# Hybrid pooling and mLSTM block on one core: pool weights folded into the input projection, gates stacked, row broadcasts in one matmul

## What is computed

```python
h = rms_norm(x, norm_g) * (1 + scale) + shift            # scale, shift, gate from silu(c) @ w_ada + b_ada
proj = h @ w_in                                          # 1024 x (7 * 512 + 8): u, z_pool, q, k, v, o, z_mlstm, gates
pool_out = causal_pool_mixer(u, w_pool, ls_pool) * silu(z_pool)
q, k = split(silu(causal_depthwise_conv(proj_qk)))
hm = mlstm_chunkwise(q, k, v, ig, lf)                    # 4 heads of 128, chunks of 128 positions
hm = hm * rsqrt(mean(hm * hm) + EPS) * mh_norm_g
mix = concat([pool_out, hm * sigmoid(o) * silu(z_mlstm)])
out = rms_norm(x + gate * (mix @ w_out), final_g)
```

## Time and profile before

| quantity | value |
|---|---|
| median of 3 runs | 2010.35 us (2009.97 to 2011.29) |
| profiled execution, its own time | 2011.44 us |
| span of its trace, first to last instruction | 2009.7 us |
| mean granted TensorE clock | 0.99 |
| PE busy | 1906.6 us (95%) |
| DVE busy | 1061.0 us (53%) |
| ACT busy | 469.8 us (23%) |
| POOL busy | 248.1 us (12%) |
| HBM read, written | 271.63 MB, 46.14 MB |

### The profile page before, as it was taken

One profiled execution on the slowest core, in us unless ns is written; L12 is line 12 of the kernel. 1 busy time (PEld: TensorE's weight loads), 2 busy tenths in 40 slices (PEclk: granted clock), 3 DMA queues, 4 the chain that ended last, 5 costly groups with the idle time before them and its releaser, 6 DMA issues.

```text
span 2009.7 us, 26240 instructions
## 1 busy us (share of the span) xinstructions
PE 1906.6 (95%) x9121; PEld 1554.7 (77%) x9121; DVE 1061.0 (53%) x2346; ACT 469.8 (23%) x979; POOL 248.1 (12%) x222
## 2 busy tenths in 40 slices
PE   2797799999999999999999999999999999999998
PEld 1585588788878888788877888778887888778886
DVE  7774476453754357362664527543474626545272
ACT  1232332112222122221222222211222122222221
POOL 0433322000030001200021000300012000210000
PEclk9998899999999999999999999999999999999999
DMA  8676562455225551456414553255513564245421
GB/s 286 205 245 198 197 232 72 161 197 200 95 92 193 192 186 53 150 193 209 148 66 154 193 197 110 91 185 195 188 64 130 196 209 147 84 142 194 168 84 63
DMA packets 120889, 319.58 MB, mean 159 GB/s; under 512 B 11356, under 2 KB 48948, under 8 KB 120756
## 3 DMA queue, kind: packets, MB, share of 16 engines
q1 hardware_dynamic: 120756, 317.81, 46.5%
HBM read 271.63 MB, written 46.14 MB: 158 GB/s over the span
## 4 chain that ended last, share of the span: by engine, by line
issue 52%; PE 21%; DVE 15%; DMA 5%; POOL 2%; ACT 1%; SPq 1%; DVEq 0%; POOLq 0%; ACTq 0%
PE ps_acc L407 5%; PE ps_acc L408 5%; PE ps_acc L409 5%; DMA sb_x_in<-x 2%; DVE sb_dmat L967 2%; DVE sb_k_w L967 1%; DMA sb_x_res<-w_out 1%; DVE sb_x_res L1370 1%; DMA sb_x_res<-x 1%; DVE sb_x_res L1383 1%; POOL sb_h_rs L873 1%; DMA out<-sb_x_res 1%; DVE sb_x_in L949 1%; DVE sb_acc_cv L1177 1%; DVE sb_mixm_lo L1284 1%
## 5 line engine op out<-in xcount | busy, mean ns | idle before, releaser
L407 PE MATMUL ps_acc<-sb_hT_hi,sb_w_split 128*128 128x512 f32 x1536 | 609.8, 397 | 28.1 <-DVE sb_oz L1194 16.1
L409 PE MATMUL ps_acc<-sb_hT_hi,sb_w_split 128*128 128x512 f32 x1536 | 603.4, 393 | 0.0
L408 PE MATMUL ps_acc<-sb_hT_lo,sb_w_split 128*128 128x512 f32 x1536 | 603.0, 393 | 0.0
L407 PEld LDWEIGHTS ps_acc<-sb_hT_hi,sb_w_split 128*128 128x128 f32 x1536 | 292.0, 190 | 90.4 <-DVE sb_oz L1194 17.8
L409 PEld LDWEIGHTS ps_acc<-sb_hT_hi,sb_w_split 128*128 128x128 f32 x1536 | 291.4, 190 | 62.6
L408 PEld LDWEIGHTS ps_acc<-sb_hT_lo,sb_w_split 128*128 128x128 f32 x1536 | 292.2, 190 | 58.7
L873 POOL TENSOR_TENSOR sb_h_rs<-sb_h_var,sb_mhalf 128x4 f32<-128x4 f32 x32 | 32.4, 1013 | 1149.7 <-DVE sb_h_var L1249 1149.7
L1177 DVE SCALAR_TENSOR_TENSOR sb_acc_cv<-sb_shifted,sb_par,sb_acc_cv 128x512 f32<-128x512 f32 x192 | 146.5, 763 | 6.8
L407 PE MATMUL ps_acc<-sb_wo_hi,sb_mixm_hi 128*128 128x512 f32 x256 | 107.0, 418 | 6.8 <-DVE sb_x_res L1370 3.5
L407 PE MATMUL ps_acc<-sb_wo_hi,sb_mixp_hi 128*128 128x512 f32 x256 | 101.1, 395 | 0.0
L408 PE MATMUL ps_acc<-sb_wo_lo,sb_mixp_hi 128*128 128x512 f32 x256 | 101.1, 395 | 0.0
(11 more groups left out here) (205 smaller groups left out, 2782.4 us busy)
## 6 DMA issues: line engine op xcount, KB each, us to landing
sb_w_split<-w_kept SPq DMA_DIRECT2D x392, 512.0 KB, 3.3
w_kept<-sb_w_split SPq DMA_DIRECT2D x56, 512.0 KB, 4.5
sb_x_res<-x SPq DMA_DIRECT2D x34, 512.0 KB, 5.7
out<-sb_x_res SPq DMA_DIRECT2D x32, 512.0 KB, 2.7
sb_x_in<-x SPq DMA_DIRECT2D x30, 512.0 KB, 5.7
sb_w_raw<-w_in SPq DMA_DIRECT2D x56, 256.0 KB, 3.4
sb_qT<-w_ada SPq DMA_DIRECT2D x4, 1024.0 KB, 6.4
sb_kT<-w_ada SPq DMA_DIRECT2D x4, 1024.0 KB, 5.4
```

What stands on the lines that cost most here:

```text
L407: pe.matmul(dst, st_hi, mv_hi, start=start, stop=False)
L408: pe.matmul(dst, st_hi, mv_lo, start=False, stop=False)
L409: return pe.matmul(dst, st_lo, mv_hi, start=False, stop=stop)
```

## The change

Five things change together.

1. The u columns of w_in are multiplied by w_pool once, in block 0 (the mean runs over positions, the map over channels, so the map can come first). Eight pieces f, two to a group: SP loads 256 KB of w_in (`load_fold`), PE turns four 128 x 128 blocks (`fold_transposed`, after tile 7+f) and multiplies them by w_pool (`fold_product`, after tile 8+f), ACT and DVE make the high and the low part, SP writes both to `w_kept` (`keep_fold`). In all blocks the u units then come from there, in block 0 too. `pool_map` goes away on PE, and `y_mixed(j)` reads the window sums straight from SBUF, in the same chunk, right after silu of zp(j). The tables TASK, SCO and the number of DVE steps follow.
2. In DVE's order `m_mixed(j-1)` comes after `y_mixed(j)` at the end of chunk j, and `y_low(j-1)` before `windows(j)`; on PE `hm_transposed(j-1)` comes after tile zp(j).
3. The gates' weights lie high beside low as 16 columns, and 16 matmuls a block replace 24; DVE adds the two halves.
4. A broadcast is one matmul of 512 columns: DVE lays out m and inter for the four heads side by side, each row kept only under its own head (`m_wide`, `inter_wide`, with `head_mask`), and a column of `chunk_sel` sums the four rows of chunk j.
5. The heads' output has a buffer of its own (it was `q_in`); `w_pool` lies in `q_in` and the raw gate weights in `v` until they are used; the ring has 5 slots, not 6; the loads of w_out stand six units earlier in SP's queue, and one load fewer stands between the first store of a block and the last load of the next block's x.

```diff
-RING = 6
+RING = 5
-hm = q_in
+hm = sb("hm", [P, NH, P])
-wpool = sb("wpool", [P, NH, P])
+wpool = q_in
...
+            def load_fold(f):
+                if f >= 2:
+                    sp.wait_ge(fold_T, f - 1)
+                off = OFF_U + P * (f // 2)
+                sp.dma_start(fold_raw[f % 2].rearrange("p (k n) -> p k n", n=P),
+                             w_in_v[:, 4 * (f % 2):4 * (f % 2) + 4, off:off + P]).then_inc(fold_loaded[f % 2], 16)
+            def keep_fold(f):
+                m = U_UNITS[f]
+                sp.wait_ge(fold_lo, f + 1)
+                for n, t in enumerate((mixm_hi, mixm_lo)):
+                    sp.dma_start(w_kept[m][:, n, :], t[:, f % 2, :, :].rearrange("p h t -> p (h t)").bitcast(F32)).then_inc(
+                        fold_kept[f % 2], 16)
...
-                wout_units = {V_UNITS + 2 * (WOUT_TILE + k) + 10: k for k in range(2, KT)} if first else {}
+                wout_units = {V_UNITS + 2 * (WOUT_TILE + k) + 4: k for k in range(2, KT)} if first else {}
...
-                        keep_w(m - RING + 1)
-                        load_raw(m)
+                        if m - RING + 1 in RAW_NO:
+                            keep_w(m - RING + 1)
+                        if m in RAW_NO:
+                            load_raw(m)
+                        else:
+                            f = U_UNITS.index(m)
+                            if m - RING in RAW_NO:
+                                kept_wait(m - RING)
+                            sp.wait_ge(fold_kept[f % 2], 32 * (f // 2 + 1))
+                            load_w(b, m)
+                        if m - 26 in range(2 * KT) and m % 2 == 0:
+                            load_fold((m - 26) // 2)
+                        if m - 33 in range(2 * KT) and m % 2 == 1:
+                            keep_fold((m - 33) // 2)
...
-                    for m in (UNITS + 2, UNITS + 3, UNITS + 4, UNITS + 5):
+                    for m in range(UNITS + 1, UNITS + RING):
                         load_w(b, m)
                     load_x(b + 1, 2)
                 store(b, 0)
                 if not last:
                     load_w(b, UNITS)
-                    load_w(b, UNITS + 1)
                     load_x(b + 1, 3)
...
-                    last = split3(sco[0:8, :], wg_hi[:, k, :], wg_lo[:, k, :], hT_hi[:, k, :], hT_lo[:, k, :],
-                                  k == 0, k == KT - 1)
+                    pe.matmul(sco[0:16, :], wg_split[:, k, :], hT_hi[:, k, :], start=k == 0, stop=False)
+                    last = pe.matmul(sco[0:16, :], wg_split[:, k, :], hT_lo[:, k, :], start=False, stop=k == KT - 1)
...
+                def fold_transposed(f):
...
+                    for i in range(4):
+                        last = pe.transpose(num[0][:, chunk(i)], fold_raw[f % 2][:, chunk(i)], ident)
+                def fold_product(f):
+                    pe.wait_ge(fold_T_copied, f + 1)
+                    if f:
+                        pe.wait_ge(fold_lo, f)
+                    for i in range(4):
+                        last = pe.matmul(num[1][:, chunk(i)], fold_turned[:, i, :], wpool[:, f // 2, :], start=True, stop=True)
...
-                    for h in range(NH):
-                        last = pe.matmul(bro[:, chunk(h)], col(row_sel, NH * j + h), m_hl[:, :], start=True, stop=True)
-                    last.then_inc(bro_full, 1)
+                    pe.matmul(bro[:, :], col(chunk_sel, j), m_wide[:, :, :].rearrange("p h t -> p (h t)"),
+                              start=True, stop=True).then_inc(bro_full, 1)
...
-                    if j > 0:
-                        pool_map(j - 1)
-                        hm_transposed(j - 1)
                     inter_rows(j)
                     tile("zp", j)
+                    if j > 0:
+                        hm_transposed(j - 1)
                     numerator_and_update(j)
-                pool_map(3)
...
+                for src, wide in ((m_row[0:16, :], m_wide), (inter_row, inter_wide)):
+                    step(V.tensor_tensor(wide[0:16, :, :], src.unsqueeze(1).broadcast_to([16, NH, P]),
+                                         head_mask[:, :].unsqueeze(2).broadcast_to([16, NH, P]), ALU.mult))
...
-                    V.scalar_tensor_tensor(silu_zp[:, :], src[:, :], ls2[:, g:g + 1], silu_zp[:, :], ALU.mult,
+                    V.scalar_tensor_tensor(silu_zp[:, :], acc_cv[:, HALO:], ls2[:, g:g + 1], silu_zp[:, :], ALU.mult,
...
-                        y_mixed(j - 1)
-                        m_mixed(j - 1)
...
-                    windows(j)
                     if j > 0:
                         y_low(j - 1)
+                    windows(j)
...
+                    y_mixed(j)
+                    if j > 0:
+                        m_mixed(j - 1)
                     if j >= 2 and not last_block:
                         prep_scale(b + 1, j - 2)
```

More of the change, by code:

```diff
@@ L91, in unit0 @@
     return V_UNITS + 2 * TILES.index((name, i))
+U_UNITS = [unit0("u", g) + half for g in range(4) for half in range(2)]
+RAW_UNITS = [m for m in range(UNITS) if m not in U_UNITS]
+RAW_NO = {m: n for n, m in enumerate(RAW_UNITS)}
+FOLD_TILE = 7
 def build(nc, x, c, norm_g, w_ada, b_ada, w_in, b_gates, conv_w, conv_b, w_pool, ls_pool, mh_norm_g,
@@ L463, in w_wait @@
                 def w_wait(m):
-                    if first:
-                        pe.wait_ge(w_lo_done, m + 1)
+                    if first and m in RAW_NO:
+                        pe.wait_ge(w_lo_done, RAW_NO[m] + 1)
                     else:
@@ L536, in one_block @@
                         gate_broadcast()
+                    if first and 0 <= t - FOLD_TILE - 1 < 2 * NH:
+                        fold_product(t - FOLD_TILE - 1)
+                    if first and 0 <= t - FOLD_TILE < 2 * NH:
+                        fold_transposed(t - FOLD_TILE)
                 def heads_to_scores(j):
@@ L563, in inter_rows @@
                     bro_wait(5 + 2 * j)
-                    for h in range(NH):
-                        last = pe.matmul(bro[:, chunk(h)], col(row_sel, NH * j + h), inter_hl[:, :],
-                                         start=True, stop=True)
-                    last.then_inc(bro_full, 1)
+                    pe.matmul(bro[:, :], col(chunk_sel, j), inter_wide[:, :, :].rearrange("p h t -> p (h t)"),
+                              start=True, stop=True).then_inc(bro_full, 1)
                 def numerator_and_update(j):
+                    if first and j == 0:
+                        pe.wait_ge(fold_lo, 2 * NH)
                     pe.wait_ge(sco_free, b * S_USES + (SCO["qk", j] + 1))
@@ L772, in one_block @@
                             wout_high(t - WOUT_TILE - 1)
+                    if first and 0 <= t - FOLD_TILE - 1 < 2 * NH:
+                        fold_high(t - FOLD_TILE - 1)
+                    if first and 0 <= t - FOLD_TILE < 2 * NH:
+                        fold_turn(t - FOLD_TILE)
                 def squares(j):
@@ L1390, in one_block @@
                 update_c(3)
-                y_mixed(3)
                 head_var(3)
```

125 lines of the change are left out of this document (85 added, 40 removed).

## The result

The changed kernel takes 1954.5 us (median of 4 runs, 1953.2 to 1955.8), against 2010.8 us for the kernel before in the same sessions: ratio 0.9718, 95% interval 0.9702 to 0.9733. The forecast was 1950.5, with a range from 1928 to 1978. The profiled execution took 1954.6 us with a span of 1952.7 us, so 57.0 us less than the span before.

The account below looks back on a forecast made before the run. PE was taken to bound seven blocks, weight traffic the first. Six loop blocks 36 us, the last 6.5 and block 0 17 sum to 59.5 off the profiled 2011.4, so a median of 1950.5 us, range 1928 to 1978.

Parts of the forecast that it names:

- Pool map, gates: On PE in each block: no pool map saves 3.44 us, 16 gate matmuls instead of 24 save 1.84 us.
- Broadcasts: On PE, eight times a block: one wide matmul of 0.24 us replaces four taking 0.48, saving 1.9 us a block.
- What DVE gives back: In chunks 2 and 3 PE waits for DVE, losing 0.5 and 1.4 us of each block's gain.
- The block's turn: Per block, out_m(1) no longer waits for y_mixed(3), 0.5 us; one weight load fewer on SP's queue, about 0.2.
- Block 0: First block gains 17 us: 8 up to the first scores, 9 from there to out_m(1); ends 5 and 29.
- the sum for the w_out laps: Block 0's load loop: laps fall from 11.9 to 8.6 us, raw load 3.8 of it; five laps save 16.6.
- The clock in block 0: PE in block 0 was costed at 0.23 us a matmul, 24 to a tile, 5.5 us a tile.
- DVE beside POOL: In block 0 POOL's splits might stretch y_mixed by up to 1.1 us in four chunks; nothing taken, far end 4.4.
- (B): Rival: DVE keeps up everywhere, block 0's loop runs at 6.7 us; 1928 us at the far end, 1932 middle; chance 0.19.
- (C): Rival: DVE paces the chunks, block 0 stays as it was because folds' traffic fills the DMA engines; 1978 us; chance 0.13.
- (D): Rival: slower, PE waits for weight loads with five ring slots; loads needing 11.6 us would eat 60 us; chance 0.04.
- (E): Rival: the wide broadcast costs as much as four narrow ones or the pool map's pace; 1966 us at the first; chance 0.02.

Follow-up runs that it names:

- The first experiment: Changed kernel with one unused fp32 matmul of 512 columns added per chunk, ahead of the broadcast of inter: 1980.4 us, ratio 0.9847.
- the second experiment: Changed kernel with each wide broadcast made as four matmuls of 128 columns: 1967.4 us, ratio 0.978.
- the two experiments on place: Changed kernel with an extra fp32 matmul per chunk, ahead of the broadcast of inter (1980.4 us) or at the chunk's end (1967.1 us).
- the eighth experiment: Kernel before with only the w_out loads six units earlier in SP's queue, ring of six, no fold: 2002.0 us, ratio 0.9945.
- the fourth: Changed kernel with ACT's high part of w_out ahead of the split of the second unit: 1949.4 us, ratio 0.9691.
- the ninth experiment: Changed kernel with an unused fp32 matmul of 512 columns at each chunk's end, behind the memory update: 1967.1 us, ratio 0.9782.
- the tenth: Changed kernel with a ring of four slots, not five: 1967.1 us, ratio 0.9781.
- the edits: Changed kernel with five edits of order (w_out's high part, out_m(1), m_mixed, y_low(3), y_high(3) each moved earlier): 1929.8 us, ratio 0.9595.

## Why the prediction was right, and where its steps were off

The sum held (57.0 us against 59.5), and the mechanisms that it named are in the trace. That it held so closely is partly luck: block 0 fell 6.3 us short and the seven later blocks gave 3.8 more. Term by term:

- **Pool map, gates:** as costed. The chunks have no pool map left (L587 before); the gates' 16 matmuls give 1.8 us a block, and the stretch from the first V matmul to the first scores shrank by just that, so the mask work on DVE cost nothing there, as taken. The first experiment pays 26 us for the pool map's work put back where it stood, with DVE's chain pushed.
- **Broadcasts:** right in effect. The wide one holds PE for 0.31 us and not for the 0.24 taken, but the matmul behind it is 0.05 us shorter: 0.22 us saved where 0.24 were forecast. Chunk 0, where on PE only the two broadcasts changed, went from 15.85 to 15.39 us, 0.23 each, and the second experiment gives 0.2 each.
- **What DVE gives back:** right in size for chunk 3 (20.43 us, forecast 20.4) and for chunk 1 (15.88, forecast 15.8). Chunk 2 took 16.86 instead of 16.3. The step there took DVE's chain as one that runs by itself from heads to heads; the two experiments on place show that PE's broadcast releases it in the middle, and its last rows show silu 0.88 us later than in chunk 1 (measured from the transposed heads), because the low part of m and prep_var stand ahead of it there.
- **The block's turn:** 0.5 + 0.2 us forecast, 1.9 measured. Besides out_m(1), the wait for the loop's turn fell from 0.90 to 0.26 us and one for the residual sum (0.31 us) is gone; 0.4 us I could not assign. This excess and the shortfall of chunk 2 go opposite ways, which is why the loop came out near its forecast; nothing in the sum provided for that.
- **Block 0:** the step that failed is the sum for the w_out laps, "lands in 3.8 us": 5.1 to 7.4. That the loop closes where it was said to was right. 10.7 us came instead of 17. By the eighth experiment the order of SP's queue alone gives as much up to out_m(1). The change is 4.6 us behind it at the first scores and makes that up in the chunks; the same stretch of block 3, where no raw unit is split in either kernel, shrank by 3.5 us (72.9 to 69.4), so that at most about 1 us of it can come from the raw u units. The 69.4 us taken for the chunks of block 0 were 70.8.
- **The clock in block 0:** the prediction took 0.23 us a matmul, 5.5 us a tile, and this is not what PE did there in the kernel before. After a wait of about 4 us for a gated tile the matmuls start 0.43 us apart, the lower of the clock's two levels (1.2 GHz), for a part of the tile:

```profile
190.70 0.80 PE L407 MATMUL ps_acc<-sb_hT_hi,sb_w_split 128*128 128x512 f32 x1 [4.35 <-DVE sb_oz L1194]
...
191.30 0.63 PE L408 MATMUL ps_acc<-sb_hT_lo,sb_w_split 128*128 128x512 f32 x1
...
191.72 0.63 PE L409 MATMUL ps_acc<-sb_hT_hi,sb_w_split 128*128 128x512 f32 x1
```

From 170 to 235 us the granted clock was 0.80 before, 0.84 in the eighth experiment, 0.92 in the change and 1.00 in the fourth: with shorter waits PE runs more of its tiles at the upper level (2.4 GHz). This is a part of what shorter laps give, and no run separates it from them.

- **DVE beside POOL:** y_mixed was to be stretched by up to 1.1 us in each of four chunks of block 0, and I took nothing. DVE's rows show it once in four; the first is chunk 1, the second chunk 2:

```profile
261.16 0.75 DVE L1367 SCALAR_TENSOR_TENSOR sb_silu_zp<-sb_acc_cv,sb_ls,sb_silu_zp 128x512 f32<-128x512 f32 x1
...
278.50 1.66 DVE L1367 SCALAR_TENSOR_TENSOR sb_silu_zp<-sb_acc_cv,sb_ls,sb_silu_zp 128x512 f32<-128x512 f32 x1
```

POOL was splitting a unit at that moment, from 278.35 to 279.61 us:

```profile
278.35 1.26 POOL L946 TENSOR_TENSOR sb_w_split<-sb_w_raw,sb_w_split 128x512 fp32r<-128x512 f32 x1
```

The 0.9 us lie on the path there, where the scores of chunk 3 in block 0 wait for m_mixed:

```profile
280.94 1.16 PE L620 MATMUL ps_sco<-sb_qT,sb_kT 128*128 128x128 f32 x8 [2.15 <-DVE sb_oz L1382]
```

The Trainium skill, "SBUF — State Buffer", section "Who interferes with whom", says that a DVE operation with two SBUF inputs contends with a GpSimd operation that reads SBUF; these rows agree, at a fifth of the 4.4 us that the prediction set as its far end.

Of the rivals, PE's pace everywhere (B) is refuted by the two waits and the ninth experiment, DVE's pace everywhere with an unchanged block 0 (C) by chunks 0 and 1 and by the laps, the ring (D) by PE's list, which names no load of a unit in the loop, and by the tenth, where four slots cost the loop nothing, and the broadcast that costs as much as four (E) by the second.

## What to carry to other kernels

When work leaves the busiest engine, look in each stage at who ends it next: here the same 0.86 us of PE cost 26 us over the kernel ahead of a broadcast that DVE waits for, and 13 us at the chunk's end. A wait that is moved away from one place tends to come up behind the next chain (heads, then y_low, then its high part on ACT); of the 25 us that the edits paid in all, 5 are block 0's, and the last 9 came only once all of that chain's orders were turned. For a loop through a queue, take each load's time from the load in that place of the queue, not from the median of its kind.

## What the runs showed that was not expected

A 512-column fp32r matmul between others of another shape held PE for 0.31 us, while the same size in a row of its kind starts every 0.23 us; what four narrow ones cost more than it shows only with the matmul behind them, 0.22 us and not 0.17. And a raw load of 256 KB took 5.1 to 5.3 us, and at times 6.4 to 7.4, behind two transfers of 512 KB issued within the microsecond before it, in the change and in the kernel before with that order of its queue; the median of 3.8 us lay between loads of about 3 and of about 4.3 us. Last, PE's granted clock fell with its waits in block 0, so that a wait cost more than its own length.
